# Low parts of the dense experts' weight tiles: two of three on VectorE instead of every other one

## The chip, the cores and the metric

The kernel runs on one core of a Trainium2 chip. The metric is the device time of one execution in microseconds (us); the figure of a kernel is the median of its runs. The engines are named as in the profile: PE is TensorE, PEld its weight loads, DVE is VectorE, ACT is ScalarE, POOL is GpSimd, SP is SyncE, which here only issues DMAs.

## What is computed

Two transformer-like blocks on 512 tokens of width 1024. The part that matters here is the feed-forward layer of the first block, a product-key mixture of 16384 experts: each token scores all experts by two small sets of keys, keeps 16 experts for each of 8 heads, and sums their outputs.

```python
g = jax.nn.softmax(top_s, axis=-1)
u = u_tab[eidx]
act = jax.nn.gelu(jnp.einsum('chkd,cd->chk', u, xb).astype(jnp.float32), approximate=False)
w = (g * act).astype(xb.dtype)
return jnp.einsum('chk,chkd->cd', w, v_tab[eidx])
```

The results must be good to about float32, so the kernel splits each float32 operand into a high part (rounded to the type that PE takes) and a low part (what the rounding left off), and makes each product in three passes: high by high, high by low, low by high.

## The kernel before, in words

**Dense experts.** For 368 of the 512 tokens the kernel doesn't gather expert rows; it multiplies those tokens by all 16384 experts, and the weight of an expert that a token did not choose is zero. The experts stand in 16 groups of 8 blocks of 128. For a group n, `U` products (n, i) give the activations of block i, `gelu` and the routing weights turn them into the weights of block i, and `V` products (n, m) multiply the eight blocks by the V table and add the result to column m of the hidden state `h`. The activations of nine of the groups were made in an earlier stage, while the routing was computed, and were spilled to DRAM: for them only the load of `a_scratch` is left here. So while V of group n runs, group n+1 is prepared either from spilled activations (call these eight-product stretches **spilled**) or by eight U products in between (sixteen products, **computed**). The whole stage is 184 products. Group n+1 is computed for n = 1, 3, 6, 8, 10 and 13; the stretches of n = 2, 4, 5, 7, 9, 11, 12 and 14 are spilled ones.

**A weight tile's way.** Every product takes one tile of 128x1024 weights from the stream `wstream`. Tile 100 belongs to product 0 of the stage, tile 283 to product 183. SP loads tile n into one of four buffers `wraw` (L2892) as soon as the low part of tile n-4 has been made. ACT casts it to the high part `wh` (L1334) when PE is done with tile n-3, since there are three buffers of `wh` and `wl`. Then `wl` = `wraw` - `wh` is made by POOL (L2716) or by DVE (L1921); which of them is told by `on_vector(n)` (L464). `product` on PE waits for `wh` and `wl` of its tile and makes 24 matmuls: eight blocks of rows by three passes (L515, L516, L517), each 128 by 368.

**The order on the engines** is written out by hand as one loop over the products. In the step of product p each engine handles the tile of product p+2:

- DVE, step of a V product: the low part of the tile of p+2 if it is DVE's (`split_lo`, L1924), then `h` += the product (L2445, waits for PE), then the low part `WTL` of a block's weights of group n+1 (`low_part`, L1921), then its *picks*. In the step of a U product: the low part of the tile of p+2, the *gate* (activation times routing weight, L2430), then picks. For a spilled block there is no product, only the gate.
- A pick is the work on one gathered expert row: for the other 144 tokens rows of the U and V tables are fetched by indirect DMAs that POOL issues (L2842) into six buffers `fetched`, and DVE multiplies or adds each (L2374, L2379, L2386, L2394). They are dealt out to the products by a table, 1 or 2 a product.
- ACT: the cast `wh` of the tile of p+2, gelu (L1666), and the high part `WTH` of a block's weights (L1656), which waits for DVE's gate. At the start of a spilled stretch its order is: `wh` for V 1, `WTH` of block 0, `wh` for V 2, `WTH` of block 1, `wh` for V 3, and so on.
- POOL: the low part of the tile of p+2 if it is POOL's, then the fetches for the picks of this step plus a lookahead of four. A fetch waits until DVE has picked the row whose buffer it takes.

A block's `WTL` on DVE and a tile's `wl` on either engine are the same operation, a subtraction of two tiles in SBUF; `low_of(n)` names the semaphore that tells of tile n, and PE and SP wait on it.

Of the kernel before, what the change touches and what calls it, by code (L numbers as in the profile page):

```python
# [58 lines left out]
W_IN, W_OUT, W_Q, W_SPILL, W_EXP = 0, 12, 20, 28, 28 + 8 * SPILLED  # L59
W_IDX = W_EXP + 8 * (N_GROUPS - SPILLED) + 8 * N_GROUPS  # L60
# [82 lines left out]
def build_program(nc, hT, wstream, gains, consts, trig, w_uq, w_ukv, keys, w_uk, w_uv, w_rg, u_rows, v_rows, out):  # L143
# [319 lines left out]

    def on_vector(n):  # L464

        return n < 3 or W_EXP + 10 <= n < W_IDX and n % 2 == 1

    def low_of(n):
        return (w_lo_dve if on_vector(n) else w_lo).at(n)
# [1419 lines left out]
    def vector(dve):  # L1889
# [33 lines left out]
        def split_lo(n):  # L1923
            if on_vector(n):  # L1924
                dve.wait_ge(*w_hi.at(n))
                minus_high(wl[n % NSPLIT][:, :], wraw[n % NRAW][:, :], wh[n % NSPLIT][:, :]).then_inc(*w_lo_dve.tell(n))
# [785 lines left out]
    def gpsimd(pool):  # L2712
# [5 lines left out]
        def split_lo(n):  # L2718
            if n >= N_TILES:
                return  # L2720
            s, r = n % NSPLIT, n % NRAW
            if on_vector(n):
                return
            pool.wait_ge(*w_hi.at(n))
            minus_high(wl[s][:, :], wraw[r][:, :], wh[s][:, :]).then_inc(*w_lo.tell(n))
# [422 lines left out]
```

## Time and profile before

| | us |
|---|---|
| median of 3 runs | 2053.56 (2052.78 to 2054.57) |
| the profiled execution, its own time | 2052.81 |
| its span, first to last instruction | 2050.9 |
| PE busy | 2017.1 (98%) |
| DVE busy | 1510.8 (74%) |
| POOL busy | 1050.3 (51%) |
| ACT busy | 994.0 (48%) |

The granted TensorE clock was 0.997 of full speed over the span, so it plays no part here. The stage of the dense experts runs from about 703 us to 1454 us of the span; the tiles that the change speaks of, 110 to 283, are used from 743 us on. Matmuls are pipelined in the profile: one lasts 0.33 us and the next starts 0.17 us after it, so a wait of PE shows as idle time that is 0.17 us shorter than the time that the product lost. Idle time of an engine that is not the bottleneck costs nothing; what counts is which wait ends last before PE goes on. The instruction that waits for several semaphores is PE's sequencer's, so PE's waits for a low part stand in the trace as "issue".

### The profile page before, as it was taken

How to read it: one execution, taken by the hardware profiler on the slowest of the kernel's cores; microseconds unless marked ns; L12 is line 12 of the kernel's file. 1: busy time of each engine (PE TensorE's matmuls, PEld its weight loads, DVE VectorE, ACT ScalarE, POOL GpSimd, SP SyncE). 2: the span in 40 equal slices, each digit the busy share in tenths (PEclk: the TensorE clock that was granted, in tenths of full speed). 3: DMA queues.
4: the chain of work that ended last, by engine and by line, in shares of the span. 5: the costliest groups of instructions: out<-in, count | busy, mean ns of one | idle time of the engine just before them, and what ended most of it. 6: DMA issues, size and time to landing. Idle time of an engine off the chain costs nothing.

```text
span 2050.9 us, 31764 instructions
## 1 busy us (share of the span) xinstructions
PE 2017.1 (98%) x11815; PEld 1803.5 (88%) x11815; DVE 1510.8 (74%) x2840; ACT 994.0 (48%) x1825; POOL 1050.3 (51%) x615
## 2 busy tenths in 40 slices
PE   9999999999999999999999999999999999999998
PEld 8746789999999999999999999999867787877777
DVE  6237538979898479999989999997687644067863
ACT  4337433367789743333333333334456642255643
POOL 3213456764455577786766676673434444411242
PEclk9999999999999999999999999999999999999999
DMA  5330224776678899999999999996312222210021
GB/s 205 81 100 12 74 91 161 253 248 226 226 256 290 312 361 374 384 386 373 362 361 356 387 376 393 357 395 205 120 62 93 92 84 103 97 37 31 21 83 62
DMA packets 152855, 435.31 MB, mean 212 GB/s; under 512 B 14464, under 2 KB 62720, under 8 KB 150528
## 3 DMA queue, kind: packets, MB, share of 16 engines
q1 hardware_dynamic: 111232, 282.29, 38.9%
q0 software_dynamic: 41472, 151.01, 19.6%
q8 instruction: 95, 1.56, 0.3%
q14 instruction: 56, 0.46, 0.1%
HBM read 391.28 MB, written 41.97 MB: 211 GB/s over the span
## 4 chain that ended last, share of the span: by engine, by line
PE 85%; DVE 9%; issue 2%; ACT 2%; DMA 1%; POOL 0%; SPq 0%; DVEq 0%; ACTq 0%
PE bank L515 18%; PE bank L516 17%; PE bank L517 17%; PE bank L921 4%; PE bank L922 4%; PE bank L923 4%; PE bank L902 3%; DVE wide L2394 2%; PE bank L1143 2%; PE bank L690 1%; PE wide L1166 1%; PE wide L1154 1%; PE bank L1166 1%; PE wide L648 1%; PE bank L784 1%
## 5 line engine op out<-in xcount | busy, mean ns | idle before, releaser
L2716 POOL TENSOR_TENSOR wl<-wraw,wh 128x1024 fp32r<-128x1024 f32 x272 | 673.5, 2481 | 709.4 <-ACT wh L1334 707.8
L1334 ACT CAST wh<-wraw 128x1024 fp32r<-128x1024 f32 x360 | 375.1, 1045 | 159.8 <-PE bank L517 130.1
L515 PE MATMUL bank<-XH,wh 128*128 128x368 f32 (+2 forms) x976 | 344.6, 353 | 1.3 <-issue 1.2
L515 PE MATMUL bank<-WTH,wh 128*128 128x368 f32 x1024 | 337.7, 330 | 7.4 <-issue 7.4
L516 PE MATMUL bank<-XL,wh 128*128 128x368 f32 (+2 forms) x976 | 340.8, 349 | 0.0
L517 PE MATMUL bank<-XH,wl 128*128 128x368 f32 (+2 forms) x976 | 339.5, 348 | 0.0
L516 PE MATMUL bank<-WTL,wh 128*128 128x368 f32 x1024 | 336.8, 329 | 0.0
L517 PE MATMUL bank<-WTH,wl 128*128 128x368 f32 x1024 | 336.7, 329 | 0.0
L515 PEld LDWEIGHTS bank<-XH,wh 128*128 128x128 f32 x976 | 183.4, 188 | 23.6 <-issue 5.5
L921 PE MATMUL bank<-XH,wh 128*128 128x368 f32 x576 | 196.4, 341 | 7.6 <-ACT ijgT L1578 2.6
L515 PEld LDWEIGHTS bank<-WTH,wh 128*128 128x128 f32 x1024 | 192.4, 188 | 10.5 <-issue 10.5
L516 PEld LDWEIGHTS bank<-XL,wh 128*128 128x128 f32 x976 | 183.2, 188 | 18.5 <-issue 2.2
L517 PEld LDWEIGHTS bank<-XH,wl 128*128 128x128 f32 x976 | 183.5, 188 | 16.4
L2842 POOL DMA_INDIRECT fetched<-in_u_rows,diag x144 | 163.3, 1134 | 65.4 <-DVE fetched L2374 42.7
L517 PEld LDWEIGHTS bank<-WTH,wl 128*128 128x128 f32 x1024 | 192.4, 188 | 0.0
L516 PEld LDWEIGHTS bank<-WTL,wh 128*128 128x128 f32 x1024 | 192.4, 188 | 0.0
L922 PE MATMUL bank<-XL,wh 128*128 128x368 f32 x576 | 191.7, 333 | 0.0
L923 PE MATMUL bank<-XH,wl 128*128 128x368 f32 x576 | 191.1, 332 | 0.0
L2842 POOL DMA_INDIRECT fetched<-in_v_rows,diag x144 | 150.6, 1046 | 39.9 <-issue 31.6
L2394 DVE SCALAR_TENSOR_TENSOR wide<-fetched,diag,wide 128x1024 f32<-128x1024 f32 x127 | 162.9, 1283 | 8.9 <-DMA fetched<-in_v_rows,diag 5.0
L921 PEld LDWEIGHTS bank<-XH,wh 128*128 128x128 f32 x576 | 109.4, 190 | 11.0 <-issue 10.0
L1921 DVE TENSOR_TENSOR wl<-wraw,wh 128x1024 fp32r<-128x1024 f32 (+1 forms) x92 | 110.2, 1198 | 2.7 <-ACT wh L1334 2.5
(552 smaller groups left out, 3860.5 us busy)
## 6 DMA issues: line engine op xcount, KB each, us to landing
wraw<-in_wstream SPq DMA_DIRECT2D x360, 512.0 KB, 5.1
g_scratch<-gs SPq DMA_DIRECT2D x12, 2048.0 KB, 8.9
gr<-g_scratch SPq DMA_DIRECT2D x15, 1536.0 KB, 11.1
a_scratch<-tmp SPq DMA_DIRECT2D x72, 184.0 KB, 2.8
tmp<-a_scratch SPq DMA_DIRECT2D x46, 184.0 KB, 7.7
sq<-a_scratch SPq DMA_DIRECT2D x26, 184.0 KB, 7.8
shifted<-hc_scratch SPq DMA_DIRECT2D x12, 270.0 KB, 4.7
fetched<-in_u_rows,diag POOLq DMA_INDIRECT x144, 7.7
```

The lines of the kernel that those rows point to most:

```text
L515: pe.matmul(o, w1, x1, start=n == 0, stop=False)
L516: pe.matmul(o, w1, x2, start=False, stop=False)
L517: m = pe.matmul(o, w2, x1, start=False, stop=n == len(ks) - 1)
L902: mm = pe.matmul(bank[:, i * 128:i * 128 + 128], hots[q % 4][1][:, i, :], hots[q % 4][0][:, i, :], start=True, stop=True, skip_group_check ...
L921: pe.matmul(o, w1s[:, c:c + 128], XH[:, k, FETCH + EXTRA:S], start=k == 0, stop=False)
L922: pe.matmul(o, w1s[:, c:c + 128], XL[:, k, FETCH + EXTRA:S], start=False, stop=False)
L923: mm = pe.matmul(o, w2s[:, c:c + 128], XH[:, k, FETCH + EXTRA:S], start=False, stop=k == KT - 1)
L1334: act.copy(wh[n % NSPLIT][:, :], wraw[n % NRAW][:, :]).then_inc(*w_hi.tell(n))
L1921: return dve.tensor_tensor(lo, src, hi.bitcast(F32), ALU.subtract)
L2394: dve.scalar_tensor_tensor(wide[1][:, :], flat, eweight[:, s:s + 1], wide[1][:, :], ALU.mult, ALU.add).then_inc(*picked.tell(("v", s)))
L2716: return pool.tensor_tensor(lo, src, hi.bitcast(F32), ALU.subtract)
L2842: pool.indirect_dma_start(fetched[buf][:, :], None, u_rows if what in ("u", "u2") else v_rows, bass.IndirectOffsetOnAxis(ap=(eidx if what ...
```

## The change

Only the rule that says which engine makes a tile's low part changes:

```diff
     def on_vector(n):
 
-        return n < 3 or W_EXP + 10 <= n < W_IDX and n % 2 == 1
+        return n < 3 or W_EXP + 10 <= n < W_IDX and n % 3 != 1
```

W_EXP is 100 and W_IDX 284. Of the 174 tiles from 110 to 283 DVE made the 87 odd ones; now it makes 116, all but 112, 115, 118 and so on, and POOL makes 58. 58 tiles go from POOL to DVE (the even ones but for 112, 118, ...) and 29 from DVE to POOL (115, 121, 127, ...). Everything else, the place of the low part in each engine's step included, stays.

On DVE at the end of the computed stretch n = 1 and the start of the spilled stretch n = 2. Before; the first `wl` is tile 133, the second tile 135, and `h` comes from V (1,7), V (2,0) and V (2,1):

```order
L1921 TENSOR_TENSOR wl<-wraw,wh 128x1024
L2445 TENSOR_TENSOR h<-bank,h 128x368
L2374 SCALAR_TENSOR_TENSOR fetched,diag<-fetched,wide 128x1024
L2430 TENSOR_TENSOR sq<-sq,gr 128x384
L2430 TENSOR_TENSOR tmp<-tmp,gr 128x384
L2445 TENSOR_TENSOR h<-bank,h 128x368
L1921 TENSOR_TENSOR WTL<-sq,WTH 128x368
L1921 TENSOR_TENSOR WTL<-tmp,WTH 128x368
L2374 SCALAR_TENSOR_TENSOR fetched,diag<-fetched,wide 128x1024
L2430 TENSOR_TENSOR tmp<-tmp,gr 128x384
L1921 TENSOR_TENSOR wl<-wraw,wh 128x1024
L2445 TENSOR_TENSOR h<-bank,h 128x368
```

The same place in the changed kernel:

```order
L1921 TENSOR_TENSOR wl<-wraw,wh 128x1024
L2445 TENSOR_TENSOR h<-bank,h 128x368
L1921 TENSOR_TENSOR WTL<-sq,WTH 128x368
L2374 SCALAR_TENSOR_TENSOR fetched,diag<-fetched,wide 128x1024 x2
L2445 TENSOR_TENSOR h<-bank,h 128x368
L2374 SCALAR_TENSOR_TENSOR fetched,diag<-fetched,wide 128x1024
L2430 TENSOR_TENSOR sq<-sq,gr 128x384
L2430 TENSOR_TENSOR tmp<-tmp,gr 128x384
L1921 TENSOR_TENSOR wl<-wraw,wh 128x1024
L2445 TENSOR_TENSOR h<-bank,h 128x368
L1921 TENSOR_TENSOR WTL<-sq,WTH 128x368
L1921 TENSOR_TENSOR WTL<-tmp,WTH 128x368
```

The first `wl` is now tile 132, which POOL made before, at the step of V (1,6); tile 133 has gone to POOL, and tile 134, for V (2,2), has come to DVE and stands between the two gates and the `h` of V (2,0). Tile 135 stays where it was.

On POOL in the computed stretch n = 1, whose rows are low parts and fetches of rows. Before:

```order
L2716 TENSOR_TENSOR wl<-wraw,wh 128x1024
L2842 DMA fetched<-in_u_rows,diag 128x1024 x2
L2716 TENSOR_TENSOR wl<-wraw,wh 128x1024
L2842 DMA fetched<-in_u_rows,diag 128x1024 x4
L2716 TENSOR_TENSOR wl<-wraw,wh 128x1024
L2842 DMA fetched<-in_u_rows,diag 128x1024 x3
```

The same place in the changed kernel:

```order
L2716 TENSOR_TENSOR wl<-wraw,wh 128x1024
L2842 DMA fetched<-in_u_rows,diag 128x1024 x3
L2716 TENSOR_TENSOR wl<-wraw,wh 128x1024
L2842 DMA fetched<-in_u_rows,diag 128x1024 x6
L2716 TENSOR_TENSOR wl<-wraw,wh 128x1024
L2842 DMA fetched<-in_u_rows,diag 128x1024 x5
```

Up to six fetches now follow each other with no low part, and so no wait for ACT's cast, between them.

## Rows read from the trace of the kernel before

**Rows 1.** Busy time by stretch: length, PE, PEld, DVE, ACT, POOL; sum: 768 to 1422.
```profile
834.00:866.00 32.00, 30.98 (x186) 30.71 (x186) 31.10 (x49) 12.77 (x17) 21.59 (x16) 1.00 1.02 400
866.00:929.00 63.00, 63.00 (x379) 63.00 (x378) 57.78 (x88) 22.72 (x31) 51.39 (x35) 1.00 1.00 385
...
sum 654.00, PE 646.59 PEld 643.37 DVE 613.12 ACT 236.24 POOL 455.44; mean PE 46.19 PEld 45.96 DVE 43.79 ACT 16.87 POOL 32.53
```

**Rows 2.** Timeline: PE's ten waits of the stage; start, length, [idle before, releaser].
```profile
840.35 0.41 PE L515 MATMUL bank<-WTH,wh 128*128 128x368 f32 x1 [1.02 <-issue]
969.54 0.41 PE L515 MATMUL bank<-WTH,wh 128*128 128x368 f32 x1 [0.74 <-issue]
1067.65 0.41 PE L515 MATMUL bank<-WTH,wh 128*128 128x368 f32 x1 [0.76 <-issue]
1116.59 0.41 PE L515 MATMUL bank<-WTH,wh 128*128 128x368 f32 x1 [0.55 <-issue]
1149.40 0.41 PE L515 MATMUL bank<-WTH,wh 128*128 128x368 f32 x1 [0.31 <-issue]
1167.20 0.41 PE L515 MATMUL bank<-WTH,wh 128*128 128x368 f32 x1 [1.55 <-issue]
1171.79 0.40 PE L515 MATMUL bank<-WTH,wh 128*128 128x368 f32 x1 [0.35 <-issue]
1264.51 0.41 PE L515 MATMUL bank<-WTH,wh 128*128 128x368 f32 x1 [0.27 <-issue]
1297.61 0.41 PE L515 MATMUL bank<-WTH,wh 128*128 128x368 f32 x1 [0.85 <-issue]
1395.20 0.41 PE L515 MATMUL bank<-WTH,wh 128*128 128x368 f32 x1 [1.00 <-issue]
```

**Rows 3.** Timeline at the first of these waits, by engine: DVE, ACT, POOL, PE.
```profile
836.22 0.55 DVE L2430 TENSOR_TENSOR tmp<-tmp,gr 128x384 f32<-128x384 f32 x1
...
837.14 0.53 DVE L1921 TENSOR_TENSOR WTL<-sq,WTH 128x368 fp32r<-128x368 f32 x1
838.21 2.43 DVE L1921 TENSOR_TENSOR WTL<-tmp,WTH 128x368 fp32r<-128x368 f32 x1 [0.55 <-ACT WTH L1656]
...
836.74 1.05 ACT L1334 CAST wh<-wraw 128x1024 fp32r<-128x1024 f32 x1
...
837.87 2.38 POOL L2716 TENSOR_TENSOR wl<-wraw,wh 128x1024 fp32r<-128x1024 f32 x1 [2.81 <-ACT wh L1334]
...
839.00 0.33 PE L517 MATMUL bank<-WTH,wl 128*128 128x368 f32 x1
```

**Rows 4.** DVE's two-tile subtractions and gates, 725 to 1445 us: busy, mean ns.
```profile
L1921 DVE TENSOR_TENSOR wl<-wraw,wh 128x1024 fp32r<-128x1024 f32 x87 | 106.3, 1221 | 2.5 <-ACT wh L1334 2.5
...
L1921 DVE TENSOR_TENSOR WTL<-tmp,WTH 128x368 fp32r<-128x368 f32 x72 | 76.7, 1067 | 5.5 <-ACT WTH L1656 3.6
...
L2430 DVE TENSOR_TENSOR tmp<-tmp,gr 128x384 f32<-128x384 f32 x72 | 54.0, 755 | 5.5 <-ACT tmp L1666 5.3
L1921 DVE TENSOR_TENSOR WTL<-sq,WTH 128x368 fp32r<-128x368 f32 x48 | 43.3, 904 | 1.7 <-ACT WTH L1656 0.5
L2430 DVE TENSOR_TENSOR sq<-sq,gr 128x384 f32<-128x384 f32 x48 | 34.7, 727 | 1.6 <-ACT sq L1666 1.4
```

**Rows 5.** POOL's low parts, 725 to 1445 us.
```profile
L2716 POOL TENSOR_TENSOR wl<-wraw,wh 128x1024 fp32r<-128x1024 f32 x90 | 226.0, 2512 | 157.8 <-ACT wh L1334 157.5
```

**Rows 6.** Timeline of a step inside a spilled stretch: POOL's low part of tile 138, DVE's gate.
```profile
851.47 2.74 POOL L2716 TENSOR_TENSOR wl<-wraw,wh 128x1024 fp32r<-128x1024 f32 x1 [2.22 <-ACT wh L1334]
...
852.99 1.63 DVE L2430 TENSOR_TENSOR sq<-sq,gr 128x384 f32<-128x384 f32 x1
```

**Rows 7.** Timeline: DVE's low part of tile 249 and PE's start of its product.
```profile
1308.42 1.22 DVE L1921 TENSOR_TENSOR wl<-wraw,wh 128x1024 fp32r<-128x1024 f32 x1
1309.56 0.53 DVE L2445 TENSOR_TENSOR h<-bank,h 128x368 f32<-128x368 f32 x1
...
1309.74 0.41 PE L515 MATMUL bank<-WTH,wh 128*128 128x368 f32 x1
```

**Rows 8.** Waits, 725 to 1445 us: total, times, longest.
```profile
ACT wh L1334 <- DMA wraw<-in_wstream: 1.7, 2, 0.9
```

## The prediction

> **What bounds the kernel now.** I read the busy times by stretch first. From 768 to 1422 us, the stretches n = 1 to 14, PE is busy 646.59 of 654 us [rows 1]: PE sets the pace, and what any change of the low parts can give back is what PE waits. DVE is nearly as full: 613.12 of 654 us, so 40.9 us idle, but unevenly. In the spilled stretch from 834 it is busy 31.10 of 32 us, in the computed one from 866 it is busy 57.78 of 63 [rows 1]. A spilled stretch leaves DVE 0.9 us, a computed one 5.2.
>
> Then I read PE's timeline for its waits. There are ten of any size, together 7.4 us idle [rows 2]. A matmul lasts 0.33 us but the next starts 0.17 after it, so each wait costs 0.17 more than its idle time: at the first, the last matmul starts at 839.00 [rows 3], the next could at 839.17 and does at 840.35 [rows 2], 1.18 us lost for 1.02 idle. Ten waits cost 7.4 + 1.7 = 9.1 us, 0.44% of the run. That is the ceiling of a direct gain.
>
> What ends them is seen at the first [rows 3]. PE is about to take tile 134 for V (2,2). ACT could not cast it before it had made the `WTH` of block 0, which waited for DVE's gate; the cast runs 836.74 to 837.79, POOL's low part 837.87 to 840.25, and PE starts 0.10 later. Counting products from the start of the stage gives the tile of each wait, in the order of [rows 2]: 134, 166, 190, 202, 210, 214, 215, 238, 246, 270. All but 215 are even, so POOL's, and seven are for V (n,2), the tile whose cast stands behind block 0's `WTH` at the start of a spilled stretch (202 and 210 are in the computed stretch n = 8).
>
> The third thing to see is that the two engines get in each other's way. DVE's `WTL` takes 0.53 us at 837.14 and 2.43 at 838.21, when it starts inside POOL's low part, and it ends 0.4 us after POOL does [rows 3]. A gate takes 0.55 [rows 3], or 1.63 beside POOL's tile 138 [rows 6].
>
> **The change, part by part.**
>
> *Low parts, own cost.* 29 more tiles on DVE. One takes 1.22 us [rows 4], and the next operation starts 1.14 after it [rows 7], so 29 x 1.14 = 33 us of DVE; POOL loses 29 x 2.51 = 73 us [rows 5], which nobody waits for as such, since POOL idles 157.5 us for ACT's casts [rows 5].
>
> *Blocking that goes.* Over 725 to 1445 us `WTL` and gates would take 0.53 and 0.55 us each unblocked [rows 3]. In [rows 4] they take 76.7 + 43.3 us for 72 + 48 `WTL`, 56.4 too much, and 54.0 + 34.7 for as many gates, 22.7 too much. 79 us for POOL's 90 tiles [rows 5] is 0.88 us a tile. 29 tiles fewer give DVE 29 x 0.88 = 25.5 us back. Net DVE gains 33 - 25.5 = 7.5 us of work. In a spilled stretch the exchange is closer still: the tile costs 1.14 on DVE and 1.63 - 0.55 = 1.08 on POOL [rows 6]. So the net work falls in the six computed stretches, about 1.2 us each against 5.2 idle [rows 1], and I cost it at nothing. If that cover were gone it would be all of the 7.5 us. The Trainium skill, "SBUF — State Buffer" (Summary: rules for kernel authors), has it that a DVE operation with two SBUF inputs and a GpSimd operation that reads SBUF exclude each other, the later one waiting for the end of the first. By that alone a dropped tile could relieve DVE of as much as POOL's 2.4 us, 29 x 2.4 = 70 us, and DVE would come out ahead. The rows agree with the rule for one pair but show 0.88 us as the mean, so the sum goes by the rows.
>
> *Waits that go.* With n % 3 the tiles 134, 246, 270 and 210 come to DVE. For 134 DVE would reach the subtraction after the second gate, at 836.77 (836.22 + 0.55), wait for the cast until 837.79, and end at about 839.07, where PE can use it at 839.17. So a DVE low part removes the wait just so. The second of idle DVE time before it is not new: in the trace DVE then sat 0.55 us and was blocked 1.9 [rows 3], and both go. Idle 1.02 + 0.85 + 1.00 for the three V (n,2), + 0.31 for 210, + 4 x 0.17: **3.9 us less**.
>
> *Waits that stay.* 166, 190, 202, 214, 238 are 1 modulo 3 and stay on POOL: 0.74 + 0.76 + 0.55 + 1.55 + 0.27 + 5 x 0.17 = 4.7 us. 215 is DVE's before and after (0.35 + 0.17 = 0.5). I take them as they are. In four of these stretches the two tiles ahead, V (n,0) and V (n,1), are now both DVE's, just before the gate that the chain hangs on: between 1.14 us later and, with the blocking of the tile taken away, nothing or better. I take nothing and keep the other end for the range.
>
> *Waits that come back.* Where PE no longer waits, it reaches the next tiles of that stretch 1.0 to 1.2 us sooner, and DVE does not. Tile 249 ends at 1309.64 and PE takes it at 1309.74 [rows 7]: no slack. PE gains 0.85 + 0.17 = 1.02 at tile 246 three products earlier, DVE perhaps 0.2 with the blocking gone; so **0.8 us back**. For the other two such stretches I take nothing; their bound is the same 1.0 us each.
>
> *Moved the other way.* 29 odd tiles go to POOL. They are mostly those that POOL can start right after the cast, and 2.4 to 2.7 us [rows 3, 6] fit into the two products, 8 us, that lie between. POOL's fetches now run up to six in a row; a fetch still waits for its buffer, so rows come a little sooner at most. SP loads tile n+4 when the low part of n is told, so a later low part is a later load; ACT waited for a load only 1.7 us in all [rows 8], and a DVE tile at a spilled step ends about when POOL's did. Nothing for both.
>
> **Sum.** 2052.81 for the profiled execution - 3.9 + 0.8 = 2049.7. The median of the runs shown is 0.75 above that execution, so the forecast for the median is **2050.5 us**, 0.15% less.
>
> **The rivals.**
>
> *No net change.* What is taken off POOL comes back on DVE: every spilled stretch stays as long as DVE's work, and the wait at V (n,2) moves to V (n,3) or the next stretch. For it: spilled stretches leave DVE 0.9 us, and the exchange is 1.14 for 1.08. Against: the wait at V (n,2) is a chain through POOL's 2.4 us. The 3.9 return: 2053.6 us. In the Trainium skill, "Perfetto Trace Analysis" (Optimizing Scalar/DVE Operations) says that moving work between these two engines might not help, as they share a read port; by that rule the sum would be this rival's.
>
> *All of POOL's waits shrink.* If the 29 odd tiles that POOL now makes run beside picks, which aren't blocked, they cost DVE little. Then the blocking that goes is that of all 58 tiles, 58 x 0.88 = 51 us against 33, DVE is ahead by 18 us in 14 stretches, over 1 us each, and the gates that the waits at V (n,2) hang on come earlier by that. The five that stayed would then lose most of their 4.7, and 215 and 249 don't wait. 2053.56 - 8.6 = 2045.0 us. For it: in the first computed stretch POOL's tiles all fall on V steps, where `WTL` stands; odd ones would be U steps. Against: in spilled stretches every step has a gate and a `WTL`.
>
> *DVE becomes the bound.* The place is the spilled stretch: eight steps with 5.33 DVE tiles for 4, so 1.52 us more of DVE work with 0.9 free. If POOL's remaining tiles block for longer than now, because DVE has more subtractions to be caught, nothing is relieved, and eight such stretches cost 8 x 1.52 = 12.2 us, less the 3.9: 2061.9 us. Each 0.1 us of relief missing per tile costs 8 x 1.33 x 0.1 = 1.1 us; from the forecast the run gets slower than before by 0.2% when 0.68 is missing, so when a dropped POOL tile relieves less than 0.4 us of DVE. For it: DVE's idle time there; against: 1.08 at the typical step. Its likely time, half the relief gone, is 2050.5 + 5.9 = 2056.4, its far end 2061.9.
>
> That the rule does not reach the tiles is excluded: the order of the instructions shows the moved rows.
>
> **How the numbers follow.** A measurement of this kernel tells about 0.2% (4.1 us) from no change. Chances: forecast 0.42, no net change 0.20, all waits shrink 0.22, DVE the bound 0.16. The forecast's own range is 2048 to 2053; with the rivals, and 1 us of run-to-run spread, 2045 to 2057 holds eight in ten. Faster by 0.2% means under 2049.4: the whole of the third case and a sixth of the forecast, 0.29. Slower means over 2057.7: half of the last case and a little of its neighbours, taken up to 0.13 for mechanisms that no row shows. The same: 0.58.
>
> **What would show it.** In the changed profile: PE's waits at tiles 134, 246, 270 and 210 gone and those at 166, 190, 202, 214, 238 of about the same size; 116 low parts on DVE in this stage's tiles at 1.2 us; `WTL` and gates together some 25 us shorter; DVE idle about 7 us less between 768 and 1422. Wrong would be: PE waits at odd tiles or at V (n,4) and V (n,6) whose low parts DVE ends late (the bound has moved); the five POOL waits gone too (the lag of DVE fell); `WTL` and gates as long as before (nothing relieved).

## The result and the profile after

| | before | after |
|---|---|---|
| median of 6 runs, us | 2054.57 (2052.78 to 2055.52) | 2063.56 (2062.26 to 2064.09) |
| ratio, 95% interval | | 1.0041, 1.0031 to 1.0052 |
| profiled execution, us | 2052.81 | 2063.22 |
| its span, us | 2050.9 | 2061.3 |

The change costs 9 us. The forecast was 2050.5 and its range ended at 2057.0: wrong in sign and outside the range. The run came out near the far end of the rival "DVE becomes the bound" (2061.9). That is chance: the loss does not lie where that rival puts it, as will be seen.

Busy times of the whole span, on the page of the kernel after (engine, us, share):

```profile
PE 2021.3 (98%) x11815; PEld 1804.7 (88%) x11815; DVE 1525.3 (74%) x2869; ACT 993.0 (48%) x1825; POOL 986.0 (48%) x586
```

DVE has 14.5 us more than the 1510.8 of before, POOL 64 less. The chain that ended last, on the page of the kernel before:

```profile
PE 85%; DVE 9%; issue 2%; ACT 2%; DMA 1%; POOL 0%; SPq 0%; DVEq 0%; ACTq 0%
```

and on that of the kernel after:

```profile
PE 73%; DVE 17%; issue 4%; DMA 3%; ACT 2%; POOL 1%; SPq 0%; DVEq 0%; ACTq 0%
```

DVE's share of the path has nearly doubled. By stretch (the view of [rows 1]: length, PE, PEld, DVE, ACT, POOL; each from DVE's `h` of the last product of one stretch to that of the next; here n = 2, n = 3, n = 13 and the sum of n = 1 to 14), the kernel after:

```profile
834.14:869.41 35.27, 34.57 (x205) 33.72 (x203) 33.14 (x52) 13.04 (x18) 19.95 (x16) 1.00 0.99 384
869.41:931.95 62.54, 62.36 (x373) 62.39 (x374) 62.24 (x90) 22.20 (x31) 43.24 (x32) 1.00 1.00 384
...
1329.07:1398.20 69.13, 67.48 (x401) 66.59 (x401) 64.60 (x65) 22.47 (x32) 47.82 (x36) 1.00 0.97 363
...
sum 665.10, PE 651.40 PEld 645.59 DVE 627.50 ACT 235.86 POOL 398.76; mean PE 46.53 PEld 46.11 DVE 44.82 ACT 16.85 POOL 28.48
```

The fourteen stretches grew from 654.0 to 665.1 us. The six computed ones grew from 386.1 to 395.6, the eight spilled ones only from 267.9 to 269.5. The stretches are timed on DVE, so a stretch in which DVE falls behind PE is long without any wait of PE in it. All busy times of the six computed stretches, before and after (length, then PE, PEld, DVE, ACT, POOL):

```profile
sum 386.07, PE 385.21 PEld 384.42 DVE 358.04 ACT 136.32 POOL 295.90; mean PE 64.20 PEld 64.07 DVE 59.67 ACT 22.72 POOL 49.32
...
sum 395.64, PE 393.46 PEld 392.05 DVE 371.37 ACT 137.49 POOL 264.54; mean PE 65.58 PEld 65.34 DVE 61.90 ACT 22.91 POOL 44.09
```

DVE has 13.3 us more to do there, and the stretches are 9.6 us longer. The idle time of DVE, on which the forecast leaned, is nearly gone in n = 3 (busy 62.24 of 62.54 us, where it was 57.78 of 63 [rows 1]), but over the six it only falls from 28.0 to 24.3 us. PE's larger waits, from the timeline of the kernel after (start, length, [idle before, releaser]):

```profile
869.59 0.41 PE L515 MATMUL bank<-XH,wh 128*128 128x368 f32 x1 [0.59 <-issue]
...
972.17 0.41 PE L515 MATMUL bank<-WTH,wh 128*128 128x368 f32 x1 [1.16 <-issue]
...
1070.15 0.41 PE L515 MATMUL bank<-WTH,wh 128*128 128x368 f32 x1 [0.64 <-issue]
...
1168.42 0.41 PE L515 MATMUL bank<-WTH,wh 128*128 128x368 f32 x1 [1.79 <-issue]
...
1269.13 0.40 PE L515 MATMUL bank<-WTH,wh 128*128 128x368 f32 x1 [2.41 <-issue]
...
1310.89 0.41 PE L515 MATMUL bank<-WTH,wh 128*128 128x368 f32 x1 [0.74 <-issue]
...
1315.98 0.41 PE L515 MATMUL bank<-WTH,wh 128*128 128x368 f32 x1 [0.84 <-issue]
...
1386.59 0.41 PE L515 MATMUL bank<-WTH,wh 128*128 128x368 f32 x1 [1.09 <-issue]
...
1404.62 0.41 PE L515 MATMUL bank<-WTH,wh 128*128 128x368 f32 x1 [1.79 <-ACT wh L1334]
...
1413.60 0.41 PE L515 MATMUL bank<-WTH,wh 128*128 128x368 f32 x1 [0.74 <-issue]
```

Their tiles: 141, 166, 190, 214, 238, 248, 249, 266, 270, 272. (Five small ones of 0.2 to 0.4 us, at 130, 139, 161, 261 and 262, and one of 0.19 at 246 are not shown.) Against [rows 2], the waits at 134, 202, 210 and 215 are gone; 166 grew from 0.74 to 1.16, 214 from 1.55 to 1.79, **238 from 0.27 to 2.41 though its tile stayed with POOL, and 270 from 1.00 to 1.79 though its tile went to DVE**. 141, 248, 249, 266 and 272 are new, and all five are tiles that DVE makes. In all there are 16 waits (13.5 us idle), where there were ten (7.4).

DVE's groups of the stage after (725 to 1455 us, groups as in [rows 4]: busy, mean ns, idle before):

```profile
L1921 DVE TENSOR_TENSOR wl<-wraw,wh 128x1024 fp32r<-128x1024 f32 x116 | 143.2, 1234 | 9.8 <-ACT wh L1334 9.8
...
L1921 DVE TENSOR_TENSOR WTL<-tmp,WTH 128x368 fp32r<-128x368 f32 x72 | 70.1, 978 | 3.3 <-ACT WTH L1656 2.1
...
L2430 DVE TENSOR_TENSOR tmp<-tmp,gr 128x384 f32<-128x384 f32 x72 | 44.9, 628 | 7.0 <-ACT tmp L1666 7.0
L1921 DVE TENSOR_TENSOR WTL<-sq,WTH 128x368 fp32r<-128x368 f32 x48 | 42.7, 893 | 1.2 <-ACT WTH L1656 0.6
L2430 DVE TENSOR_TENSOR sq<-sq,gr 128x384 f32<-128x384 f32 x48 | 32.5, 681 | 2.6 <-ACT sq L1666 2.6
```

`WTL` and gates together fell from 208.7 us [rows 4] to 190.2: 18.5 us of relief, where 25.5 was forecast. And it lies in the wrong place. Over the six computed stretches the `WTL` take 62.7 us before and 58.7 after, and the gates 26.8 and 27.8; with 16 POOL tiles fewer there, the `WTL` give back 0.25 us a tile, not 0.88. POOL's low parts (as [rows 5]):

```profile
L2716 POOL TENSOR_TENSOR wl<-wraw,wh 128x1024 fp32r<-128x1024 f32 x61 | 154.0, 2526 | 168.5 <-ACT wh L1334 167.6 <-issue 0.5
```

A remaining tile lasts as long as before (2526 against 2512 ns). POOL now waits for DVE's picks to free row buffers: 31.4 us for those of L2374, where it was 8.7, and 49.5 for those of L2394, where it was 4.2.

**One wait followed back.** Tile 238 is V (11,2), after the computed stretch n = 10. The timeline of the kernel after (DVE, then ACT, then POOL):

```profile
1261.53 0.53 DVE L2445 TENSOR_TENSOR h<-bank,h 128x368 f32<-128x368 f32 x1
1261.98 2.67 DVE L2394 SCALAR_TENSOR_TENSOR wide<-fetched,diag,wide 128x1024 f32<-128x1024 f32 x2
1264.56 1.02 DVE L2430 TENSOR_TENSOR tmp<-tmp,gr 128x384 f32<-128x384 f32 x2
...
1265.15 0.50 ACT L1656 CAST WTH<-tmp 128x368 fp32r<-128x368 f32 x1 [8.05 <-DVE tmp L2430]
1265.55 1.05 ACT L1334 CAST wh<-wraw 128x1024 fp32r<-128x1024 f32 x1
...
1266.68 2.35 POOL L2716 TENSOR_TENSOR wl<-wraw,wh 128x1024 fp32r<-128x1024 f32 x1 [4.26 <-ACT wh L1334]
```

The gates begin 4.57 us before PE's start at 1269.13. In the kernel before the same chain ran from gates at 1259.89 to PE at 1264.51, 4.62 us: it is no longer, it starts later. Counted from PE's start of V (11,0), two products ahead, the gates come 6.07 us after it (1258.49) where they came 3.81 after it (1256.08). That is 2.26 us more, and the wait lost 2.14 more. DVE entered the stretch late: `h` of the last product of n = 10 starts 3.1 us after PE is done with it, where it was 0.6. At tile 270, DVE's own now, the chain from the gates to PE has shrunk from 4.60 us (1390.60 to 1395.20) to 3.39 (1401.23 to 1404.62), which is the gain the change was to bring; but the gates come 6.56 us after PE's start of V (14,0), 2.0 later than the 4.56 of before, and the wait is longer.

### The profile page after: what moved, and what is told of

Read it like the earlier page. It is cut to its first block, busy times and chain, and to the rows that moved or that the text cites. A ratio compares the mean times of both kernels' runs of the same rounds, so it can differ in the third digit from the quotient of the medians.

```text
span 2061.3 us, 31764 instructions
## 1 busy us (share of the span) xinstructions
PE 2021.3 (98%) x11815; PEld 1804.7 (88%) x11815; DVE 1525.3 (74%) x2869; ACT 993.0 (48%) x1825; POOL 986.0 (48%) x586
## 4 chain that ended last, share of the span: by engine, by line
PE 73%; DVE 17%; issue 4%; DMA 3%; ACT 2%; POOL 1%; SPq 0%; DVEq 0%; ACTq 0%
PE bank L515 14%; PE bank L516 14%; PE bank L517 14%; PE bank L921 4%; PE bank L922 4%; PE bank L923 4%; DVE fetched L2374 3%; PE bank L902 3%; DVE wide L2394 3%; DVE WTL L1921 2%; PE bank L1143 2%; DVE wl L1921 1%; PE bank L690 1%; DMA fetched<-in_u_rows,diag 1%; DMA wraw<-in_wstream 1%
## 5 line engine op out<-in xcount | busy, mean ns | idle before, releaser
L2716 POOL TENSOR_TENSOR wl<-wraw,wh 128x1024 fp32r<-128x1024 f32 x243 | 601.5, 2480 | 716.3 <-ACT wh L1334 714.2
L2842 POOL DMA_INDIRECT fetched<-in_v_rows,diag x144 | 161.8, 1123 | 81.3 <-DVE wide L2394 47.9
L2394 DVE SCALAR_TENSOR_TENSOR wide<-fetched,diag,wide 128x1024 f32<-128x1024 f32 x127 | 162.9, 1283 | 9.1 <-DMA fetched<-in_v_rows,diag 4.6
L1921 DVE TENSOR_TENSOR wl<-wraw,wh 128x1024 fp32r<-128x1024 f32 (+1 forms) x121 | 147.1, 1216 | 10.6 <-ACT wh L1334 9.8
```

What stands on the lines that cost most here:

```text
L1921: return dve.tensor_tensor(lo, src, hi.bitcast(F32), ALU.subtract)
L2394: dve.scalar_tensor_tensor(wide[1][:, :], flat, eweight[:, s:s + 1], wide[1][:, :], ALU.mult, ALU.add).then_inc(*picked.tell(("v", s)))
L2716: return pool.tensor_tensor(lo, src, hi.bitcast(F32), ALU.subtract)
L2842: pool.indirect_dma_start(fetched[buf][:, :], None, u_rows if what in ("u", "u2") else v_rows, bass.IndirectOffsetOnAxis(ap=(eidx if what ...
```

## The experiments

"The rule" is the changed kernel's n % 3 != 1. Kernels that need it have a helper `computed_at(n)`: true for tiles whose step lies in a computed stretch. In computed stretches the odd tiles belong to steps of U products and the even ones to steps of V products (but for the two at a stretch's ends, where the order shifts by one). Medians in us; each ratio is to the kernel before on the same chip (2054.74 to 2054.93).

| run | tiles of DVE in computed / spilled stretches | median | ratio, 95% interval |
|---|---|---|---|
| e1 | every other / the rule | 2056.55 | 1.0006, 0.9997 to 1.0016 |
| e2 | the rule / every other | 2064.68 | 1.0051, 1.0037 to 1.0064 |
| e3 | every other / V (n,2) for V (n,1) | 2047.94 | 0.9967, 0.9955 to 0.9979 |
| e4 | one of three in both | 2087.01 | 1.0159, 1.0145 to 1.0173 |
| e5 | e2, low part later in the step | 2082.37 | 1.0134, 1.0117 to 1.0151 |
| e6 | before, 16 low parts made twice | 2069.30 | 1.0075, 1.0058 to 1.0092 |
| e7 | before, lighter picks | 2046.12 | 0.9958, 0.9944 to 0.9972 |
| e8 | e2, lighter picks | 2046.77 | 0.9962, 0.9948 to 0.9976 |
| e9 | the even ones / every other | 2098.17 | 1.0221, 1.0206 to 1.0236 |
| e10 | e9 and e3 | 2091.00 | 1.0176, 1.0162 to 1.0190 |
| e11 | all odd and a third of the even / every other | 2052.69 | 0.9991, 0.9982 to 1.0000 |
| e12 | e11 and e3 | 2048.24 | 0.9972, 0.9961 to 0.9983 |

**Which stretches (e1, e2).**

```diff
+        return n % 2 == 1 if computed_at(n) else n % 3 != 1     # e1
+        return n % 3 != 1 if computed_at(n) else n % 2 == 1     # e2
```

> The rule of the change for the tiles whose low part is made in spilled stretches (13 more on VectorE), the old one in computed stretches. If VectorE's queue sets the length of the whole stage and each tile that comes to it costs the same, 13/29 of the measured 9 to 10.4 us: about 4.5 us slower than before. If computed stretches cover their share, as the prediction had it, all of the loss is here: 9 to 10 us slower.

> The reverse: the rule of the change in computed stretches alone (16 more on VectorE), all ten tiles of the waits but 210 as before. If VectorE's queue sets the length everywhere: about 5.5 us slower than before. If the 5 us that VectorE idles in a computed stretch cover the new work: no difference, within 1.5 us.

e2 alone has the whole loss, 9.8 us; e1 is within what can be told from no change. Neither expectation of either run had this split. PE's waits in e1 come to 8.1 us in 12, little more than before: those at 134, 202 and 238 go, 246 and 270 shrink, 166 grows, and those at 141, 248, 249 and 272 come, 0.6 to 0.8 us idle each. In e2 (waits view, 725 to 1450 us: total, times, longest):

```profile
PE bank L525 <- issue: 15.6, 13, 3.0
```

13.2 of these 15.6 us are at the seven V (n,2), where it was 6.2 before, though their tiles are made by POOL as before. So in the spilled stretches the exchange is even, and the loss comes from the computed ones: work added there is paid at V (n,2) of the next spilled stretch.

e1 also tests the chain by itself at one place. For V (2,2) DVE starts the gates 4.6 us after PE's start of V (2,0) in both kernels, and PE goes on without a wait where it lost 1.18 us: with the gates just as late, a low part on DVE comes early enough.

**Is it V (n,2)'s chain through POOL? (e3).** V (n,2)'s tile of each spilled stretch goes to DVE and V (n,1)'s to POOL in return.

```diff
+        what, group, m = STEPS[n - W_EXP]
+        if what == "V" and m in (1, 2) and (group + 1 == N_GROUPS or ORDER[group + 1] < SPILLED):
+            return m == 2
         return n % 2 == 1
```

> The old alternation, but at the start of each spilled stretch the tile of V (n,2) goes to VectorE and that of V (n,1) to GpSimd, so that VectorE has 88 tiles instead of 87. If the waits at V (n,2) are a chain through GpSimd's 2.4 us, the seven of them go, 7.4 us with the 0.17 each, and the kernel is 5 to 7.5 us faster than before. If they only show that VectorE is behind, the waits come back at the next tiles and the time is within 1.5 us of before.

It is 7.0 us under the kernel before. The waits view of e3 (total, times, longest):

```profile
PE bank L522 <- issue: 1.8, 5, 0.5
```

7.4 us in ten waits have become 1.8 in five, none of them at the seven V (n,2). So the waits that the forecast read are there to be had. But e3 does not show that the chain through POOL alone makes them, for it also relieves DVE. V (n,1)'s low part stood just ahead of the gates, and without it these start 3.4 us after PE's start of V (n,0), where it was 4.5 (means of the seven): 1.1 us, as much as a wait cost. And the `WTL` of the eight spilled stretches, before and in e3:

```profile
sum 267.89, PE 161.83 PEld 92.24 DVE 50.84; mean PE 20.23 PEld 11.53 DVE 6.35
...
sum 265.60, PE 165.30 PEld 93.93 DVE 34.88; mean PE 20.66 PEld 11.74 DVE 4.36
```

16 us less: in each of the eight the second `WTL` took 2.4 us beside POOL's tile for V (n,2), and takes 0.53 in e3. With one low part more in all (88 for 87), DVE has 14 us less to do over the fourteen stretches (598.8 for 612.9 us).

**How much work DVE may have (e4, e6).** e4 is `n % 3 == 1`, DVE making one of three. e6 is the kernel before with 16 of DVE's low parts in the computed stretches made twice:

```diff
                 dve.wait_ge(*w_hi.at(n))
+                if n >= W_EXP + 10 and n % 3 == 1 and computed_at(n):
+                    minus_high(wl[n % NSPLIT][:, :], wraw[n % NRAW][:, :], wh[n % NSPLIT][:, :]).then_inc(*twice.tell(n))
+                    dve.wait_ge(*twice.at(n))
```

> The opposite step: VectorE makes one tile of three (58), GpSimd two. If the length follows VectorE's work, a tile that leaves it gives back what one that comes costs, 0.36 us: 10 us faster at most, limited by what TensorE waits for before (9.1), so 5 to 9 us faster. If what counts is how late GpSimd's 2.4 us come, more tiles wait for them and the kernel is 3 to 10 us slower than before.

> The kernel before with 16 of VectorE's low parts in computed stretches made twice (the second after a wait on the first), so that VectorE gets the 16 x 1.22 us of e2_computed_only and GpSimd keeps its tiles. The difference to e2 (9.8 us slower than before) is what 16 GpSimd tiles less are worth to VectorE. If a GpSimd tile blocks VectorE by 0.88 us and VectorE's time counts: 9.8 + 14 = about 24 us slower than before. If the relief is worth nothing in computed stretches: 10 to 12 us slower.

e4: fewer tiles on DVE is worse still, 32 us where the expectation had 10 at most, and it is more work for DVE: in the computed stretches its low parts fall from 58.8 to 42.2 us, but its gates rise from 26.8 to 55.9 and its `WTL` from 62.7 to 72.9. So the number of DVE's tiles does not tell its work. e6: 16 more low parts (16 x 1.14 = 18.2 us) cost 14.6 us by the medians, 10.4 in the profiled execution (2065.16), which was the quickest of four. Either way most of the work shows: the idle time of the computed stretches hides little of it. The 4.8 us between e6 and e2, which have the same low parts on DVE there, are what 16 POOL tiles less are worth in e2, 0.3 us each.

**Is it DVE's lateness? (e7, e8).** In the computed stretches each pick works on half of its row, so the picked rows' sums lack the other half. e7 is the kernel before with it, e8 is e2 with it.

```diff
-                dve.scalar_tensor_tensor(row3, row3, 1.0, tokens, ALU.mult, ALU.mult,
+                half = slice(0, KT // 2 if light[0] else KT)
+                dve.scalar_tensor_tensor(row3[:, half, :], row3[:, half, :], 1.0, tokens[:, half, :], ALU.mult, ALU.mult,
...
```

> The kernel before with half of each pick in the computed stretches left out (VectorE multiplies 512 of the 1024 columns of a row, so its output is not the whole sum): about 160 picks x 0.55 us less for VectorE there. It is the control for e8. If VectorE's lag at the end of a computed stretch makes the waits at V (n,2) that follow, five of the seven shrink or go (those of n = 2, 7, 9, 11, 14): 3 to 5 us faster than before. If those waits are the chain through GpSimd alone: no difference.

> e2_computed_only with the same halves of picks left out in computed stretches. If the 9.8 us of e2 are VectorE's lag, they go with it: the same time as e7 within 1.5 us. If they are the order of the work (casts waited for at the head of the queue, blocking by GpSimd), they stay: 8 to 10 us slower than e7.

The same within 0.65 us. With DVE ahead of its work, e2's rule costs nothing: its loss is that DVE falls behind, whatever makes it. In e8 the six stretches take 379.2 us and PE is busy for all of it.

e7 went past both of its expectations. It is 8.6 us faster than the kernel before, nearly all that PE's waits cost there, with every tile on its old engine. Its waits (as above):

```profile
PE bank L523 <- issue: 2.7, 4, 1.3
```

Five of the seven at V (n,2) are gone, though POOL makes these tiles; 214 and 270 are left with 0.42 and 0.74 us idle. So the chain through POOL is too long only where DVE is late at the gates: an earlier gate removes the wait (e7), and so does a shorter chain (e1 at V (2,2)). e3 has both.

**The low part later in the step (e5).** e2's rule, with DVE's low part moved behind the gate of a U step and behind `h` and `WTL` of a V step.

```diff
-                    split_lo(W_EXP + product_no[0] + 2)
...
+                    split_lo(W_EXP + product_no[0] + 2 - (n == 0))
```

> The rule of e2_computed_only, with VectorE's low part moved behind the other subtractions of its step (behind the gate in a U step, behind h and the low part of the block's weights in a V step). If the loss of e2 is VectorE standing still for ScalarE's cast at the head of its queue (2.5 us of such waits before, 9.8 with the change), most of it comes back: 2 to 5 us slower than before instead of 9.8. If the loss is the work itself, which leaves VectorE behind at the end of a computed stretch, it stays: 8 to 12 us slower, or more, since the low parts come later.

Much worse, by 17.7 us against e2. New waits of PE, 0.9 to 1.9 us idle, stand at the even V tiles that are DVE's (120, 132, 144, 150, 156 and so on): the low part itself is then late. The place at the front of the step is needed.

**Which tiles POOL keeps (e9, e10, e11, e12).**

```diff
+        return n % 2 == (0 if computed_at(n) else 1)                              # e9
...
+        if computed_at(n):                                                        # e11
+            return n % 2 == 1 or n % 3 == 2
+        return n % 2 == 1
```

> The old rule in spilled stretches; in computed ones the alternation turned over: VectorE makes the tiles whose step is a V step, GpSimd those of the U steps. VectorE has 87 tiles as before. If what a GpSimd tile costs VectorE hangs on the step it stands in (in a V step the low part of the block's weights is caught, in a U step mostly picks, which are not), VectorE gets back up to the 37.5 us that its gates and block low parts take too long in computed stretches before, ends them less late, and the kernel is 2 to 6 us faster than before. If a tile catches something in either step, no difference within 2 us, or slower.

> e3_third_to_vector and e9_other_parity together. If they act on different waits (e3 on the chain at V (n,2), e9 on VectorE's lag), 9 to 11 us faster than before, near all of the 9.1 us that TensorE waits. If e9 does nothing, as e3: 7 us faster. If turning the parity over makes VectorE later at the start of a spilled stretch, less than e3: 0 to 5 us faster.

> Change: only in the computed stretches; DVE keeps all 48 odd tiles and takes 16 of the even ones as well, so it makes 64 of 96 as in e2, but POOL's tiles fall on U steps 5 times, where it was 17 in e2, 6 in the kernel before and 42 in e9. My theory (the step counts: a POOL tile at a U step overlaps a subtraction of DVE for longer than one at a V step, and it is the odd tiles gone to POOL that took the relief back): the 16 tiles add 16 x 1.14 = 18.2 us to DVE and 16 tiles at V steps relieve it of about 0.8 us each, 12.8; blocked time in the computed stretches falls from 38.0 to about 25 us, net 5 us more of DVE against 16.5 in e2, and the run is 2 to 5 us above the kernel before, about 2058, clearly under e2. First rival (the number of tiles on DVE counts, and not where POOL's lie): as e2, 1.0051, about 2065, with blocked time about 36. Second rival (relief is as large as the tile costs, 1.1 us each): no change, 2054, and blocked time near 20.

> Change: e11's rule in the computed stretches and e3's exchange of V (n,1) for V (n,2) in the spilled ones. If the two act apart, e3's 7 us come off e11's time: 2051 by my theory, 2058 by the first rival, 2047 by the second. If e11 costs only through the waits at V (n,2), as e2 did, and these don't hang on POOL here, it costs less than in e11, and the time is 2048 to 2050. Under 2047.5 it would beat e3.

e9 has before's number of tiles on each engine and, against its expectation, loses 43.4 us. e11 has e2's numbers, 64 tiles of 96 on DVE, and loses nothing. What differs is how many of POOL's tiles are at U steps: 6 before, 17 in e2, 42 in e9, 5 in e11. The work of DVE over the six computed stretches, from the sums of the busy times by stretch:

| | POOL's tiles at U / V steps | DVE low parts | `WTL` | DVE busy | length of the six | idle |
|---|---|---|---|---|---|---|
| before | 6 / 42 | 58.8 | 62.7 | 358.0 | 386.1 | 28.0 |
| e11 | 5 / 27 | 78.4 | 44.6 | 357.7 | 385.2 | 27.4 |
| after | 17 / 15 | 78.1 | 58.7 | 371.4 | 395.6 | 24.3 |
| e2 | 17 / 15 | 80.2 | 56.3 | 372.4 | 395.0 | 22.7 |
| e6 | 6 / 42 | 79.7 | 62.2 | 376.9 | 400.1 | 23.2 |
| e9 | 42 / 6 | 58.9 | 100.2 | 402.5 | 427.2 | 24.7 |

Two things are to be read here. **The length follows DVE's busy time**: over 45 us of it the idle time stays between 23 and 28. It is hardly a reserve: of the 18.9 us of work that e6 adds there, 4.9 went into it. The run follows too: against the kernel before the profiled spans differ by -2.8 (e11), 10.4 (after), 11.9 (e2), 12.4 (e6) and 45.2 us (e9), the six stretches by -0.9, 9.6, 8.9, 14.0 and 41.1. **16 tiles fewer on POOL gave DVE 18.2 us of `WTL` back in e11 (1.14 each, all that they cost) and 6.5 in e2 (0.4 each)**: between the two, 12 POOL tiles moved from V to U steps took 11.7 us, 1 us each. By e9 it is 37.5 us for 36, the same, and the gates add 8.7. So the second rival on record for e11, relief as large as the cost, holds, and mine (0.8 a tile) was still too low.

The rows for it. Busy times by computed stretch of instructions that touch `WTL`, in e9 (stretch, length, PE, PEld, DVE; n = 1, n = 3, and the sum of six):

```profile
769.45:832.64 63.19, 21.08 (x65) 12.20 (x65) 4.16 (x8) 1.00 1.01 395
864.64:934.70 70.06, 23.85 (x73) 13.72 (x73) 18.64 (x8) 1.00 0.95 349
...
sum 427.16, PE 142.50 PEld 82.38 DVE 100.19; mean PE 23.75 PEld 13.73 DVE 16.70
```

and the sum in e11:

```profile
sum 385.15, PE 131.72 PEld 76.02 DVE 44.55; mean PE 21.95 PEld 12.67 DVE 7.43
```

e9's first stretch is the surprise: eight `WTL` in 4.16 us, not one of them blocked, though POOL's tiles lie on U steps there too; in n = 3 the eight take 18.64. The timeline of e9, DVE and POOL at the third product of the one and of the other:

```profile
781.24 0.53 DVE L2455 TENSOR_TENSOR h<-bank,h 128x368 f32<-128x368 f32 x1
781.69 0.98 DVE L1931 TENSOR_TENSOR WTL<-tmp,WTH 128x368 fp32r<-128x368 f32 x2
...
780.27 1.85 POOL L2852 DMA_INDIRECT fetched<-in_u_rows,diag  x1 [0.30 <-DVE fetched L2384]
782.43 1.05 POOL L2852 DMA_INDIRECT fetched<-in_u_rows,diag  x1 [0.30 <-issue]
783.50 2.41 POOL L2726 TENSOR_TENSOR wl<-wraw,wh 128x1024 fp32r<-128x1024 f32 x1
...
877.46 0.53 DVE L2455 TENSOR_TENSOR h<-bank,h 128x368 f32<-128x368 f32 x1
877.91 3.28 DVE L1931 TENSOR_TENSOR WTL<-tmp,WTH 128x368 fp32r<-128x368 f32 x1
...
876.49 1.86 POOL L2852 DMA_INDIRECT fetched<-in_u_rows,diag  x1 [0.30 <-issue]
878.38 2.41 POOL L2726 TENSOR_TENSOR wl<-wraw,wh 128x1024 fp32r<-128x1024 f32 x1
```

DVE's order is the same in both: low part, `h`, `WTL`. In the first, one more fetch stands ahead of POOL's tile, which starts at 783.50 when both `WTL` are over. In the second it starts at 878.38, inside the `WTL`, which then takes 3.28 us instead of 0.53. So a POOL tile at a U step costs DVE nothing or up to 2.7 us, by some tenths of a microsecond (of e9's 48 `WTL` in these stretches 16 take 0.53 us, 13 take 2.3 to 2.5, and 19 take 3.3). At a V step, DVE is mostly caught in part: 32 of the 48 `WTL` of the kernel before take 0.9 to 1.8 us. All that are caught end alike: of the 224 gates and `WTL` of the kernel before between 768 and 1422 us, 69 end 0.40 to 0.45 us after the POOL tile that they overlap, wherever they began. The picks, which take one operand from `wide`, held in PSUM (where PE's products land too) and not in SBUF, are not caught: 72 of them overlap a POOL tile there, and all last 1.21 to 1.29 us as the others do. That the extra fetch is what keeps the first stretch clear is read from these rows; no run tried it.

e10 takes 7.2 us off e9, as e3 takes 7.0 off the kernel before: V (n,2) and the computed stretches are separate matters there. e12 does not add e11's 2 us, which can hardly be told from none, to e3's gain; it equals e3. Of the kernels that compute the whole sums, e3 and e12 are the fastest, 2047.94 and 2048.24 us, under both the kernel before and the changed one.

## Why the prediction was wrong

**What bounds the kernel: half right.** PE's ten waits and their chain were read rightly. That the chain hangs on how late DVE is at the gate was not: with DVE ahead of its work five of the seven go by themselves (e7). And the 5.2 us that DVE idles in a computed stretch were taken for a reserve. Most of them are not. The waits of DVE from 768 to 1422 us, kernel before (total, times, longest):

```profile
DVE h L2445 <- PE bank L517: 10.2, 16, 1.7
DVE tmp L2430 <- ACT tmp L1666: 5.3, 6, 1.8
DVE wide L2394 <- DMA fetched<-in_v_rows,diag: 5.0, 6, 1.3
DVE WTL L1921 <- ACT WTH L1656: 4.1, 8, 0.6
```

and the kernel after, same stretch of time:

```profile
DVE wl L1921 <- ACT wh L1334: 7.0, 10, 1.2
DVE tmp L2430 <- ACT tmp L1666: 7.0, 5, 2.9
...
DVE h L2445 <- PE bank L517: 0.6, 1, 0.6
```

The 10.2 us in which DVE waits for PE, over fourteen stretches, are used up. The waits for ACT's casts (1.9 us before) and gelu grow instead, and all of DVE's idle time falls by no more than 3.3 us (40.9 to 37.6) where the signs of the forecast had 7. That these waits follow DVE's own lateness, and so hide nothing, is argued from their place in the order, and not shown one by one.

**The step that failed** is "So the net work falls in the six computed stretches, about 1.2 us each against 5.2 idle [rows 1], and I cost it at nothing." Both halves of it fell.

- *The net work.* In the computed stretches it is 371.4 - 358.0 = 13.3 us, 2.2 each: 19.3 us more of low parts (78.1 - 58.8) for only 4.0 less of `WTL` (the 2 us between lie in other rows). The relief of 0.88 us a tile was a mean over POOL's tiles, and was used for the difference of 58 that leave and 29 that come. The even ones that leave the computed stretches are worth 1.14 each (e11, which sends no odd tile to POOL, gets its whole cost back); the odd ones that come, "nothing" in the step *Moved the other way*, cost DVE about 1 us more than a tile at a V step.
- *The cover.* The stretches grew by 9.6 of the 13.3 us (395.6 - 386.1): idle fell only from 28.0 to 24.3. e6 shows it with nothing else changed, and e8 that the loss goes when DVE has room.

"If that cover were gone it would be all of the 7.5 us" was in the text; the range did not hold it, since the spilled stretches were thought the only place without cover.

The Trainium skill, "SBUF — State Buffer" (Summary: rules for kernel authors), says that of a DVE operation with two SBUF inputs and a GpSimd operation that reads SBUF the later one waits for the end of the first. The long `WTL` agree, 2.4 to 3.3 us against 0.53. By the records of e9 it was the first that waited: `WTL` is shown from 877.91, 0.47 us ahead of POOL's tile, and ends 0.4 us after it. The 70 us that the prediction drew from that rule would need every tile to catch a gate or `WTL` from its start; the mean of what they catch depends on where they stand.

**Waits that go: four were forecast, two went.** 134 and 210 are gone, 246 shrank (0.85 to 0.19 us idle), 270 grew. The chain did get shorter where DVE took the tile, by 1.2 us at 270; the forecast left out that its start, the gate, hangs on DVE's lateness at the end of the stretch ahead. The wait for the cast was seen, and taken as fixed.

**Waits that stay.** Of the five, 202 went, 190 is smaller, 166, 214 and 238 grew by 0.4, 0.2 and 2.1 us. 215, which was also taken as it was, went.

**Waits that come back: right in size at 249, too few.** 249 was to wait about 0.8 us and is idle 0.84 before it. But 248, in the same stretch, waits 0.74 as well, and so does 272, in one of "the other two such stretches", for which I took nothing and named 1.0 us as the bound; after the other, 141 waits 0.59. These are the prediction's own signs of being wrong: waits at odd tiles and at V (n,4) and V (13,6) whose low parts DVE ends late. So in the spilled stretches alone nothing is gained (e1: +1.6 us, not to be told from none), which was the rival "No net change".

**Costs in spilled stretches: right.** The exchange was forecast as even, 1.14 against 1.08 us. After the change the gates of the stage are 11.3 us shorter (88.7 to 77.4), all of it in spilled stretches, where DVE's work rises by 1.2 us in all and the length by 0.2 each.

**The rivals.** "DVE becomes the bound" had the sign and the mechanism (the remaining POOL tiles catch DVE for longer), but put it in the spilled stretches, with 0.9 us free, where e1 finds next to nothing; that its time came near is luck. "All of POOL's waits shrink" argued that odd tiles run beside picks, which aren't blocked, and cost little. The picks aren't, but a tile need not stay beside them: e9's first stretch does just that, and its other five show the opposite. The Trainium skill, "Perfetto Trace Analysis" (Optimizing Scalar/DVE Operations), says that moving work between these two engines might not help. Here it is worth from 43 us lost (e9) to 7 gained (e3), by which tiles move.

## What to carry to other kernels

A mean price of contention, taken over all instances, does not price a change that also moves the instances: list which operations of the one engine run beside which of the other, before and after, and give each kind its own price. Idle time of an engine inside a stage hides added work only where it lies behind that work and ahead of the next wait on it; the test is whether the stage gets longer when a little work is done twice. And where a chain hangs on one tile, give that one tile to the other engine and another back, rather than change the share of all; then see which of its two effects paid, the shorter chain or the earlier start.

## What the runs showed of the hardware that was not expected

After a long wait PE ran at half its clock for a few microseconds. The windows of the kernel after at tile 214 (stretch, length, busy of PE, PEld, DVE, ACT, POOL, then the granted clock):

```profile
1164.00:1168.00 4.00, 2.63 (x16) 2.32 (x14) 3.45 (x5) 2.80 (x4) 2.03 (x1) 1.00 1.01 425
1168.00:1170.00 2.00, 1.58 (x6) 1.61 (x7) 1.92 (x2) 0.00 (x0) 1.54 (x3) 0.71 0.99 396
1170.00:1172.00 2.00, 2.00 (x8) 2.00 (x8) 1.98 (x3) 0.20 (x1) 1.70 (x2) 0.50 1.01 376
1172.00:1174.00 2.00, 2.00 (x13) 2.00 (x12) 2.00 (x4) 1.25 (x2) 1.41 (x2) 0.94 0.99 372
```

PE was idle 1.79 us before 1168.42; from 1168.8 to 1172.2 the granted clock is 0.50, the 1.2 GHz level, and matmuls start 0.31 us apart instead of 0.17. Some eleven of them lose 0.14 each, 1.5 us on top of the wait. In the kernel before no wait of this stage was followed by this, the longest being 1.55 us idle. It doesn't follow every long one: in the kernel after the wait of 2.41 us at 1269.13 is followed by full clock. In e9, whose waits are longer (up to 5.2 us idle), stretches at the lower level follow six of them.
